# The FFN of a hybrid decoder layer reads x times the post-mixer root plus y, and x is put right later

## The reference

```
def _rms_norm(x, g):
    y = xf * lax.rsqrt(jnp.mean(xf * xf, axis=-1, keepdims=True) + EPS)
    return (y * g)
...
    x = x + _rms_norm(o @ w_out, g_post_mix)
    h = _rms_norm(x, g_pre_ffn)
    u = h @ w_gate
    up = h @ w_up
    u_pad = jnp.concatenate([prev_conv, u], axis=1)
    c = conv_b + sum(conv_w[j] * u_pad[:, j:j + L] for j in range(CONV_W))
    y = (jax.nn.gelu(c, approximate=True) * up) @ w_down
    x = x + _rms_norm(y, g_post_ffn)
```

## Time and profile before

| | us |
|---|---|
| median of 3 runs | 1158.87 (1158.53 to 1159.19) |
| the profiled execution | 1158.79 |
| its span | 1157.0 |
| PE busy | 1142.6 (99%) |
| DVE busy | 722.6 (62%) |
| ACT busy | 554.6 (48%) |
| GpSimd (POOL) busy | 141.2 (12%) |

### The profile page before, as it was taken

One profiled execution on the slowest core, in us unless ns is written; L12 is line 12 of the kernel. 1 busy time (PEld: TensorE's weight loads), 2 busy tenths in 40 slices (PEclk: granted clock), 3 DMA queues, 4 the chain that ended last, 5 costly groups with the idle time before them and its releaser, 6 DMA issues.

```text
span 1157.0 us, 24986 instructions
## 1 busy us (share of the span) xinstructions
PE 1142.6 (99%) x9612; PEld 1110.8 (96%) x9612; DVE 722.6 (62%) x1115; ACT 554.6 (48%) x880; POOL 141.2 (12%) x197
## 2 busy tenths in 40 slices
PE   9999999999999999999999999999999999999997
PEld 9998889989999999999999999999999999999996
DVE  7876767789575875656565656565656444454444
ACT  7544447576456654544444444444444333343332
POOL 0201124344011010100110011001100000020001
PEclk9999999999999999999999999999999999999999
DMA  8847775666565455555555555555555665666552
GB/s 341 276 154 254 266 282 194 215 207 208 164 183 181 139 155 198 169 194 167 196 174 188 173 190 180 183 177 186 184 179 190 207 182 182 182 183 182 183 158 76
DMA packets 60674, 222.14 MB, mean 192 GB/s; under 512 B 6904, under 2 KB 9088, under 8 KB 59536
## 3 DMA queue, kind: packets, MB, share of 16 engines
q1 hardware_dynamic: 55920, 196.53, 52.7%
q0 software_dynamic: 4560, 24.87, 6.4%
q10 hardware_dynamic: 144, 0.05, 0.0%
HBM read 216.42 MB, written 5.00 MB: 191 GB/s over the span
## 4 chain that ended last, share of the span: by engine, by line
PE 89%; DVE 6%; ACT 2%; DMA 1%; issue 1%; SPq 0%; DVEq 0%; ACTq 0%
PE ps L1341 28%; PE ps L1342 28%; PE ps L1343 27%; DVE wl L778 2%; DMA raw<-in_w_in 1%; PE ps L1492 1%; PE ps L1426 1%; PE ps L1417 1%; PE ps L1415 1%; DVE junk L925 0%; PE ps L1444 0%; ACT oBh L606 0%; PE ps L1613 0%; PE ps L1607 0%; DVE oT L958 0%
## 5 line engine op out<-in xcount | busy, mean ns | idle before, releaser
L1341 PE MATMUL ps<-hh,wh 128*128 128x264 f32 x2048 | 587.7, 287 | 0.6 <-DVE wl L778 0.3
L1343 PE MATMUL ps<-hh,wl 128*128 128x264 f32 x2048 | 581.0, 284 | 0.0
L1342 PE MATMUL ps<-hl,wh 128*128 128x264 f32 x1920 | 544.6, 284 | 0.0
L778 DVE TENSOR_TENSOR wl<-raw,wh 128x1024 fp32r<-128x1024 f32 x360 | 437.1, 1232 | 166.3 <-ACT wh L484 166.0
L484 ACT CAST wh<-raw 128x1024 fp32r<-128x1024 f32 x360 | 371.2, 1046 | 262.5 <-PE ps L1343 257.5
L1341 PEld LDWEIGHTS ps<-hh,wh 128*128 128x128 f32 x2048 | 387.3, 189 | 12.6 <-issue 11.5
L1343 PEld LDWEIGHTS ps<-hh,wl 128*128 128x128 f32 x2048 | 387.4, 189 | 0.0
L1342 PEld LDWEIGHTS ps<-hl,wh 128*128 128x128 f32 x1920 | 363.2, 189 | 0.1
L1342 PE MATMUL ps<-gg,wh 128*128 (+1 forms) x704 | 200.0, 284 | 0.0
L1341 PE MATMUL ps<-gg,wh 128*128 (+1 forms) x704 | 199.6, 283 | 0.0
L1343 PE MATMUL ps<-gg,wl 128*128 (+1 forms) x704 | 196.1, 279 | 0.0
(11 more groups left out here) (264 smaller groups left out, 950.1 us busy)
## 6 DMA issues: line engine op xcount, KB each, us to landing
raw<-in_w_gate SPq DMA_DIRECT2D x88, 512.0 KB, 3.7
raw<-in_w_up SPq DMA_DIRECT2D x88, 512.0 KB, 4.5
raw<-in_w_down SPq DMA_DIRECT2D x88, 512.0 KB, 3.6
raw<-in_w_in SPq DMA_DIRECT2D x68, 512.0 KB, 4.9
raw<-in_w_out SPq DMA_DIRECT2D x32, 512.0 KB, 3.6
K<-in_kb POOLq DMA_DIRECT2D x8, 1280.0 KB, 7.8
K<-in_vb POOLq DMA_DIRECT2D x16, 640.0 KB, 5.5
xT<-in_x SPq DMA_DIRECT2D x3, 528.0 KB, 8.5
```

The lines of the kernel that those rows point to most:

```text
L778: V.tensor_tensor(wl[:, slot], raw[:, slot], wh[:, slot].bitcast(F32), ALU.subtract).then_inc(lo_ready, 1)
L1341: nc.tensor.matmul(out, a, x, start=start, stop=False)
L1342: nc.tensor.matmul(out, a, xl, start=False, stop=False)
L1343: return nc.tensor.matmul(out, b, x, start=False, stop=stop)
```

## The change

- DVE's reciprocal of r1 is gone from the front of the FFN part. r1 goes into a tile of its own, `rms1`, and `residual` now does `xT = xT * rms1`, then `xT = xT + yT`. yT stays as it is.
- The second root needs eps times r1 squared: DVE computes it from rms1 into `rB` (new, L1067 of the changed kernel), adds it to the sums that PE left in PSUM (new, L1072; ACT's copy L712 goes) and the root is taken without eps.
- `hold_clock` has 8 dummy matmuls in place of 16.
- Behind group 0 DVE computes 1/r1 (new, in place in rms1, L1120). GpSimd then multiplies xT by it, in 8 instructions of two tiles each (`keep_x1`, L1318): four ahead of `window(1)` and four behind it.
- rms1 lies in memory that the FFN's hidden tiles take later, so ACT and DVE wait for these 8 instructions before their loop.

```diff
@@ ACT
             act.wait_ge(sum_ready, 1)
-            nc.scalar.activation(rms[:], ps[:, B_M, 0:TOK], ACT.Sqrt, bias=eps[:], scale=1.0 / D_MODEL).then_inc(norm_a, 1)
+            nc.scalar.activation(rms1[:], ps[:, B_M, 0:TOK], ACT.Sqrt, bias=eps[:], scale=1.0 / D_MODEL).then_inc(norm_a, 1)
...
             split(chunk(B_GU, 0, 8, 10))
-            act.wait_ge(sum_ready, 2)
-            nc.scalar.copy(rms[:], ps[:, B_M, 0:TOK]).then_inc(norm_a, 1)
             split(chunk(B_GU, 0, 8, 11))
             act.wait_ge(sum_ready, 3)
-            nc.scalar.activation(rms[:], ps[:, 6, 0:TOK], ACT.Sqrt, bias=eps[:],
-                                 scale=1.0 / (32 * D_MODEL)).then_inc(norm_a, 1)
+            nc.scalar.activation(rms[:], ps[:, 6, 0:TOK], ACT.Sqrt, scale=1.0 / (32 * D_MODEL)).then_inc(norm_a, 1)
...
             ffn_gate(0, 0)
             ffn_gate(1, 1)
+            act.wait_ge(x1_kept, MT // 2)
@@ DVE
             dve.wait_ge(norm_a, 1)
-            V.reciprocal(rB[:], rms[:]).then_inc(rB_ready, 1)
-            dve.wait_ge(rB_ready, 1)
...
-                line.step(V.tensor_tensor(y2, y2, wide(rB[:], j1 - j0), ALU.mult))
-                V.tensor_tensor(x2, x2, y2, ALU.add).then_inc(x1_ready, 1)
+                line.step(V.tensor_tensor(x2, x2, wide(rms1[:], j1 - j0), ALU.mult))
+                V.tensor_tensor(x2, x2, y2, ALU.add).then_inc(z_ready, 1)
...
-            for j in (8, 9, 10):
+            line.do(V.scalar_tensor_tensor(rB[:], rms1[:], EPS * D_MODEL / 4, rms1[:], ALU.mult, ALU.mult))
+            for j in (8, 9):
                 split(chunk(B_GU, 0, 8, j))
-            dve.wait_ge(norm_a, 3)
+            line.need(line.n)
+            dve.wait_ge(sum_ready, 2)
+            V.tensor_tensor(rms[:], ps[:, B_M, 0:TOK], rB[:], ALU.add).then_inc(eps_added, 1)
+            split(chunk(B_GU, 0, 8, 10))
+            dve.wait_ge(norm_a, 2)
             V.reciprocal(rB[:], rms[:]).then_inc(rB_ready, 1)
...
             ffn(0, 0)
+            V.reciprocal(rms1[:], rms1[:]).then_inc(r1_ready, 1)
             ffn(1, 1)
+            dve.wait_ge(x1_kept, MT // 2)
@@ GpSimd
+            def keep_x1(j0, j1):
+                for jj in range(j0, j1):
+                    x2 = xT[:, 2 * jj:2 * jj + 2]
+                    G.tensor_tensor(x2, x2, rms1[:].unsqueeze(1).to_broadcast([P, 2, TOK]), ALU.mult).then_inc(x1_kept, 1)
+                pool.wait_ge(x1_kept, j1)
+
             window(0)
-            with pool.Fori(0, G_FF - 1) as i:
+            pool.wait_ge(r1_ready, 1)
+            pool.wait_ge(h2l_ready, MT)
+            pool.wait_ge(sqx_ready, MT // 2)
+            keep_x1(0, MT // 4)
+            window(1)
+            keep_x1(MT // 4, MT // 2)
+            with pool.Fori(0, G_FF - 2) as i:
@@ PE
-            hold_clock(16)
+            hold_clock(8)
...
-                        pe.wait_ge(norm_a, 2)
+                        pe.wait_ge(eps_added, 1)
                         nc.tensor.matmul(ps[:, 6, 0:TOK], ones[:], rms[:], start=True, stop=True).then_inc(sum_ready, 1)
```

More of the change, by code:

```diff
@@ L310, in build @@
                 sqx = sb("sqx", [P, MT, TOK], F32, over)
+                rms1 = sb("rms1", [P, TOK], F32, over)
             sb("align_g", [P, 16], F32, ffn)
@@ L387, in build @@
         ysq_ready, ysq_used = sem("ysq_ready"), sem("ysq_used")
-        x1_ready, h2h_ready, h2l_ready = sem("x1_ready"), sem("h2h_ready"), sem("h2l_ready")
+        z_ready, h2h_ready, h2l_ready = sem("z_ready"), sem("h2h_ready"), sem("h2l_ready")
+        eps_added, r1_ready, x1_kept = sem("eps_added"), sem("r1_ready"), sem("x1_kept")
         sum_ready = sem("sum_ready")
@@ L701, in _ @@
                 for j in range(4 * q, 4 * q + 4):
-                    act.wait_ge(x1_ready, j + 1 if j < 2 else j // 2 + 2)
+                    act.wait_ge(z_ready, j + 1 if j < 2 else j // 2 + 2)
                     nc.scalar.activation(hh[:, j], xT[:, j], ACT.Copy,
@@ L1068, in _ @@
                 split(chunk(B_GU, 0, 8, 2 * q + 1))
-            for j in (8, 9, 10):
+            line.do(V.scalar_tensor_tensor(rB[:], rms1[:], EPS * D_MODEL / 4, rms1[:], ALU.mult, ALU.mult))
+            for j in (8, 9):
                 split(chunk(B_GU, 0, 8, j))
-            dve.wait_ge(norm_a, 3)
+            line.need(line.n)
[3 more added lines that the diff above has]
+            dve.wait_ge(norm_a, 2)
             V.reciprocal(rB[:], rms[:]).then_inc(rB_ready, 1)
-            dve.wait_ge(rB_ready, 2)
+            dve.wait_ge(rB_ready, 1)
             def ffn(i, at):
@@ L1135, in _ @@
                                     ALU.mult).then_inc(down_v, 1)
-            dve.wait_ge(norm_a, 4)
+            dve.wait_ge(norm_a, 3)
             line.step(V.reciprocal(rms[:, P:P + QT], rms[:, 0:QT]))
@@ L1308, in window @@
                 G.tensor_copy(state, U_dec[:, :, :, 1:3]).then_inc(u_kept, 1)
-            window(0)
-            with pool.Fori(0, G_FF - 1) as i:
+            def keep_x1(j0, j1):
[3 more added lines that the diff above has]
+                pool.wait_ge(x1_kept, j1)
+            window(0)
+            pool.wait_ge(r1_ready, 1)
[5 more added lines that the diff above has]
+            with pool.Fori(0, G_FF - 2) as i:
                 line.loop(i, 1)
-                window(i + 1)
-            line.end(G_FF - 1)
+                window(i + 2)
+            line.end(G_FF - 2)
             pool.wait_ge(u_kept, G_FF)
@@ L1725, in _ @@
             add_x(1)
-            pe.wait_ge(rB_ready, 3)
+            pe.wait_ge(rB_ready, 2)
             for bank in (6, 5):
```

## The result

| | before | after |
|---|---|---|
| median | 1158.95 us (1158.53 to 1159.19, 4 runs) | 1167.24 us (1167.07 to 1168.76, 4 runs) |
| profiled execution, its span | 1158.79, 1157.0 us | 1167.07, 1165.3 us |

The change makes the kernel slower: ratio 1.0076, 95% interval 1.0064 to 1.0088. The forecast was 1166.9 us.

A forecast was written before the change was run, and what follows sets the result against it. PE, busy 99% of the span, was taken as the bound, each FFN wait adding to the time. The terms -1.84 + 1.5 + 4.55 + 3.85 = +8.1 us on 1158.79 gave 1166.9 us, range 1162.0 to 1169.7.

The forecast's parts named there:

- the late U: Group 1: GpSimd's copy stands behind reciprocal and four multiplications, so DVE writes U at 424.85 in place of 417.44.
- the contact of the two engines: Group 1: two-input DVE instructions and GpSimd instructions exclude each other for the whole instruction, lengthening multiplications, taps and splits.
- the third wait: PE ahead of chunk 15: GpSimd's second four multiplications fall on DVE's taps, 3.85 us; without contact 0.2.
- Front: Start of the FFN part: without the reciprocal the first hh and PE's first matmul come 1.84 us earlier.
- Second sums: Second root: DVE's product of r1 with itself and addition of eps cost nothing, with 2.4 us of cover.
- First wait: PE ahead of chunk 13: DVE's reciprocal stands ahead of that chunk's split, which had 0.28 us of cover; 1.5 us.
- Second wait: PE ahead of chunk 14: four GpSimd multiplications ahead of window(1) delay U and the chunk's split; 4.55 us.
- one for one: Rival: GpSimd gets in behind every DVE instruction, fourth multiplication ahead of chunk 15's split, 1.3 us more: 1168.2; chance 0.13.
- A sign that I had named: GpSimd's L1318 was to take 1.3 us in the first four and 1.9 or more in the second four.
- The clock: Rival: the waits of 4.55 and 3.85 us bring PE's slow rate back, 2.7 us lost in chunk 15: 1169.6; chance 0.15.
- No contact: Rival: DVE passes GpSimd freely, only list order counts; waits 1.5, 3.45 and 0.2: 1162.1; chance 0.15.
- The stalls are hidden: Rival: group 1's copy is in time (U by 420.4), only the front counts: 1157.0; chance 0.04, whole or half.

The follow-up runs named there:

- e1: Changed kernel without restoring x (no reciprocal of r1 behind group 0, none of the eight multiplications, no wait for them): 1157.03 us, ratio 0.9988.
- e7: Changed kernel with x restored in the down projection, as in e6, but with 16 dummy matmuls: 1156.76 us, ratio 0.9985.
- e2: Changed kernel with the reciprocal of r1 behind group 0 kept but the eight GpSimd multiplications left out: 1158.33 us, ratio 0.9998.
- e8: Changed kernel with the reciprocal of r1 moved behind the split of chunk 13 in place of ahead of it: 1169.28 us, ratio 1.0089.
- e10: The changed kernel itself, measured again on the same chip as e8 and e9: 1168.5 us, ratio 1.0086.
- e4: Changed kernel without the second four GpSimd multiplications, so half of x is not restored: 1164.11 us, ratio 1.0046.
- e9: Changed kernel with one more GpSimd wait, so the second four multiplications begin when DVE's taps of group 1 are done: 1164.32 us, ratio 1.0049.
- e3: Changed kernel with window(1) put ahead of all eight GpSimd multiplications, nothing left out: 1164.36 us, ratio 1.005.
- e6: Changed kernel with r1 copied by ACT, and its reciprocal and the eight multiplications moved to the down projection: 1156.86 us, ratio 0.9987.
- e5: Kernel before the change with 8 dummy matmuls in place of 16, nothing else: 1159.45 us, ratio 1.001.

## Why the prediction was right, point by point

The time is right, and so are its mechanisms, the late U and the contact of the two engines; but the term of the third wait came near its forecast by luck.

*Front, -1.84:* 1.84 in the trace (1.97 less 0.13), and 1.6 in e1. The step that named the first hh as the wait that ends last was wrong (e7): the wait for the third does, and it moved by the same amount.

*Second sums, 0:* PE has no wait between the third tile of hh and chunk 13, in e1 and in the changed kernel. The new addition of eps began at 401.05, 2.4 us ahead of PE's use of the result at 403.86 (L1653), as forecast.

*First wait, 1.5:* 1.3 in the trace (417.16 against 415.73 + 0.12) and in e2. The split began 1.71 behind the start of the reciprocal, and not 1.84, and took 1.16, not 1.22. Right as a price of the reciprocal alone. As a term of the sum it stands for no cost of its own in the changed kernel (e8); the sum came out right because the terms behind it were worked out as what PE waits when it has already waited, so that together they measure the length of the chain.

*Second wait, 4.55:* 4.38, from 420.04 (417.16 + 2.88) to 424.42. From the start of chunk 13 to U it took 5.30 us; forecast were 5.50 (419.35 to 424.85).

*Third wait, 3.85:* chunk 15 was forecast for 431.66 with the front's gain taken off, and began at 431.68. By the reckoning of the sum, with chunk 14 at full speed, the term is 4.38 (431.68 less 424.42 + 2.88), 0.5 over the forecast, while the two waits before it are 0.4 under theirs together. The contact is real, but the pattern that I gave it (one multiplication, then two taps) did not occur: it was one multiplication for each tap, and the fourth fell on the split of chunk 15, as in my rival "one for one", to which I gave 0.13. The rival's 5.15 is too high by 0.8, since it lets the first multiplication go ahead of the first tap. That tap slipped in front at its old price, while GpSimd was held up with its copy beside the split of chunk 14 (L1312, 1.11 in place of the 0.19 of the same copy in group 0). So the two errors, a multiplication too few and one too early, nearly cancel, and the size of this term is luck. A sign that I had named failed for the same reason: L1318 in the second four took 1.51 to 1.60, not 1.9 or more.

*The clock:* chance 0.15 in the prediction. It fell in the first profiled execution, where the wait for chunk 15 hid it, as the rival said of chunk 14, and it fell twice in e10, where the slow part of chunk 15 cost 1.6. The rival's price of 2.7 us was too high. With a fall in every trace in which PE waited 4 us or more (after, e4, e8, e9, e10), it deserved a larger chance.
The Trainium skill (TensorE: Matmul & The Clock Gate, § What's actually happening) says that an idle engine falls back to 1.2 GHz; the trace agrees, with 0.58 in a microsecond in which PE did nothing (423 to 424) and 0.50 behind it.

*No contact:* excluded by e3, and by e4 and e9, where the taps take 1.90 as soon as no multiplication falls on them. The Trainium skill (SBUF — State Buffer, § Who interferes with whom) says that whichever of the two engines issues first has the shared port pair for its whole instruction; the trace agrees, with taps of 1.44 to 1.56 us in place of 0.5.

*The stalls are hidden:* it did not happen. Its condition was also too weak. With U at 420.4, chunk 15 comes 1.84 us late, which only uses up the front's gain and gives 1158.8; for 1157.0 U had to be written by 418.6 (chunk 15 ready at 423.57, less the 5.01 of the earlier trace rows between the two).

Single runs of e1 and e6 lie 1 to 1.5 us over their fellows. All three in e1, and the highest in e6, have spans like the others and 2.6 to 3.4 us outside the span in place of 1.8. Two of e6 have longer spans (1155.9 and 1156.1 against 1154.7 to 1155.4); their cause is left open.

## What to carry to other kernels

An instruction taken off a chain is only worth what its work does not cost where it is put again: 1.84 us were won here and ten lost, because the work went to a group whose first splits had 0.3 to 1.4 us to spare, while the down projection took the same work for nothing (e6), and the splits of 16 and 17 took half of it (e9). Before work goes to an engine with much idle time, look at what stands behind it in that engine's own list (here a copy of 0.2 us that all of group 1 waits for) and at what the other engine does with two inputs at that time. And where several waits follow each other, work out the time at which the last of them ends; to remove one of them shows whether they were one chain.

## What the runs showed of the hardware that I had not expected

GpSimd's multiplications and DVE's two-input instructions did not simply alternate in a fixed pattern: beside L1323 in the earlier trace rows two splits went ahead of one GpSimd instruction, beside the taps it was one for one. In group 1 the one tap that began while GpSimd was held up kept its price of 0.51.

The clock fell 0.4 us into the work that followed an idle time of only 2.23 us (e5, granted clock 0.58 and 0.50 in the microseconds from 376 on), and it did not fall around one of 3.06 us (e3, 1.00 from 415 to 445); so in this kernel the length of one wait does not tell by itself whether the clock falls. The same kernel lost 1.3 us more or less in its span by where in its waits the clock fell and came back (1165.3 in the first trace, 1166.6 in e10).
